# Two attention stages: gate tiles requested on ScalarE's DMA queue, five buffers in the local one, and all its low parts on GpSimd

## The reference

```
def _mixer_swa(h, positions, w_in, sinks):
    ...
    o = _banded_gqa(q, k, v, SWA_WINDOW, sinks).reshape(B, S, MIX_WIDTH)
    return o * jax.nn.silu(z)

def _mixer_mla(h, positions, w_in, q_norm, kv_norm, w_uq, w_ukv):
    ...
    o = _mla_attention(q_nope, q_rope, k_nope, k_rope, v).reshape(B, S, MIX_WIDTH)
    return o * jax.nn.silu(z)
```

## Time and profile before

| | us |
|---|---|
| median of 3 runs | 3240.16 (3235.90 to 3241.09) |
| profiled execution, its own time | 3234.05 |
| its span in the profile | 3232.2 |

### The profile page before, as it was taken

One profiled execution on the slowest core, in us unless ns is written; L12 is line 12 of the kernel. 1 busy time (PEld: TensorE's weight loads), 2 busy tenths in 40 slices (PEclk: granted clock), 3 DMA queues, 4 the chain that ended last, 5 costly groups with the idle time before them and its releaser, 6 DMA issues. The chain is left out here.

```text
span 3232.2 us, 40805 instructions
## 1 busy us (share of the span) xinstructions
PE 2960.0 (92%) x13514; PEld 2324.8 (72%) x13536; DVE 1913.8 (59%) x2771; ACT 1575.7 (49%) x2778; POOL 1244.5 (39%) x1044
## 2 busy tenths in 40 slices
PE   8999977778899999999677789999999999799998
PEld 6888875555688778888565467777777777578877
DVE  3544215444278774444555568778787787347875
ACT  3111114556444544444223167777777777544553
POOL 0022002223132541000210068888888888523353
PEclk9999988889899999999898789999999999899999
DMA  5255349664897665554567924252442522399764
GB/s 176 72 125 124 106 107 190 155 156 117 274 295 242 234 231 195 177 173 147 191 261 289 293 62 105 69 125 69 95 103 69 125 69 53 100 301 284 235 222 159
DMA packets 268849, 531.15 MB, mean 164 GB/s; under 512 B 46376, under 2 KB 94632, under 8 KB 260080
## 3 DMA queue, kind: packets, MB, share of 16 engines
q1 hardware_dynamic: 215696, 412.78, 44.5%
q10 hardware_dynamic: 52960, 116.02, 11.5%
HBM read 351.06 MB, written 177.37 MB: 163 GB/s over the span
## 5 line engine op out<-in xcount | busy, mean ns | idle before, releaser
L2161 POOL TENSOR_TENSOR mla_pl<-mla_p,mla_ph 128x512 fp32r<-128x512 f32 (+3 forms) x640 | 707.2, 1120 | 361.0 <-ACT mla_p L2023 352.5
L1324 PE MATMUL end_bank<-end_xh,end_whi 128*128 128x512 f32 x1600 | 633.1, 396 | 49.9 <-DVE end_xl L1510 28.7
L1325 PE MATMUL end_bank<-end_xl,end_whi 128*128 128x512 f32 x1600 | 625.0, 391 | 0.0
L1326 PE MATMUL end_bank<-end_xh,end_wlo 128*128 128x512 f32 x1600 | 625.0, 391 | 0.0
L1881 PE MATMUL mla_score<-mla_q,mla_k 96*128 96x512 f32 (+7 forms) x1920 | 555.7, 392 | 6.3 <-DMA mla_q<-mla_m_t 6.3
L1496 DVE TENSOR_TENSOR end_wlo<-end_wraw,end_whi 128x1024 fp32r<-128x1024 f32 x188 | 256.4, 1364 | 366.7 <-ACT end_whi L1379 366.2
L1379 ACT CAST end_whi<-end_wraw 128x1024 fp32r<-128x1024 f32 x188 | 197.2, 1049 | 552.8 <-PE end_bank L1326 516.2
L2022 ACT ACTIVATE mla_ph<-mla_score 128x512 fp32r<-128x512 f32 (+3 forms) x640 | 341.0, 533 | 225.8 <-PE mla_score L1881 222.8
L1881 PEld LDWEIGHTS mla_score<-mla_q,mla_k 96*128 96x128 f32 (+1 forms) x1920 | 362.8, 193 | 91.5 <-issue 36.8
L2053 DVE TENSOR_REDUCE mla_mx<-mla_mx 128x1 f32<-128x512 f32 (+3 forms) x640 | 371.9, 603 | 94.2 <-PE mla_mx L1881 93.6
L2099 DVE TENSOR_TENSOR mla_acc<-mla_acc,mla_p 128x512 f32<-128x512 f32 (+3 forms) x576 | 348.6, 605 | 118.6 <-ACT mla_p L2023 114.6
(11 more groups left out here) (233 smaller groups left out, 4695.7 us busy)
## 6 DMA issues: line engine op xcount, KB each, us to landing
end_wraw<-in_w_out ACTq DMA_DIRECT2D x64, 512.0 KB, 7.8
end_wraw<-in_pe_gate ACTq DMA_DIRECT2D x64, 512.0 KB, 4.8
end_wraw<-in_w_in ACTq DMA_DIRECT2D x56, 512.0 KB, 3.8
swa_q<-scratch_q_hi SPq DMA_DIRECT2D x32, 512.0 KB, 9.3
end_raw<-scratch_o SPq DMA_DIRECT2D x32, 512.0 KB, 11.7
end_factor<-scratch_inv SPq DMA_DIRECT2D x64, 256.0 KB, 10.0
scratch_proj<-end_out_f SPq DMA_DIRECT2D x64, 256.0 KB, 7.0
scratch_sum<-end_out_f SPq DMA_DIRECT2D x64, 256.0 KB, 6.5
```

Source lines behind the costliest of these rows:

```text
L1324: nc.tensor.matmul(bank, wh[:, at], xh[:, k0 + k, :], start=(k == 0), stop=False)
L1325: nc.tensor.matmul(bank, wh[:, at], xl[:, k0 + k, :], start=False, stop=False)
L1326: last = nc.tensor.matmul(bank, wl[:, at], xh[:, k0 + k, :], start=False, stop=(k == kc - 1))
L2161: pool.tensor_tensor(p_lo[b][:, off:TC], prob[b][:, off:TC], p_hi[b][:, off:TC].bitcast(F32), ALU.subtract).then_inc(p_lo_ok, 1)
```

## The change

1. The requests for gate tiles leave SP's program and go to ScalarE's. Before the first unit's work ScalarE requests the first `n_gate - 2` of them, and at the first step of a chunk c, ahead of its wait for the scores, that of chunk c + `n_gate - 3`.
2. `n_gate` is 5 in the local attention and 3 in the global one. The output tile and the denominator row keep three buffers.
3. `on_vector`, `low_part` and the second semaphore go: GpSimd makes the low part of every step in the local attention too.

```
-        small = 3
+        small, n_gate = 3, 3 if long else 5
...
-        def on_vector(g):
-            return not long and not flat[g][2]["last"]
...
-            def load_gate(c):
-                if c >= small:
-                    sp.wait_ge(gated, c - small + 1)
-                sp.dma_start(cfg["gate"](gate[c % small]), cfg["gate_src"](*chunks[c])).then_inc(gate_in[c % small], 16)
-
             load_high(0)
             load_low(0)
-            load_gate(0)
             load_high(1)
             for c in range(len(chunks)):
                 u = chunks[c][0]
-                if c + 1 < len(chunks):
-                    load_gate(c + 1)
                 if c == 0 or chunks[c - 1][0] != u:
...
-                if on_vector(g):
-                    pe.wait_ge(p_lo_v_ok, low_count[g])
-                else:
-                    pe.wait_ge(p_lo_ok, low_count[g])
+                pe.wait_ge(p_lo_ok, g + 1)
                 mm(out, v, low, False, st["last"]).then_inc(weighed, 1)
...
+            def load_gate(c):
+                if c >= n_gate:
+                    act.wait_ge(gated, c - n_gate + 1)
+                act.dma_start(cfg["gate"](gate[c % n_gate]), cfg["gate_src"](*chunks[c])
+                              ).then_inc(gate_in[c % n_gate], 16)
+
+            ahead = n_gate - 3
+            for c in range(ahead + 1):
+                load_gate(c)
             max_row(0)
             for g in range(total + tail):
                 if g < total:
...
+                    if st["first"] and c and c + ahead < len(chunks):
+                        load_gate(c + ahead)
                     act.wait_ge(scores, g + 1)
...
             for g in range(total + tail):
-                if g < total and not on_vector(g):
+                if g < total:
```

More of the change, by code:

```diff
@@ L1735, in attention_phase @@
         den_row = [s.sb(f"den_row{b}", [1, TC]) for b in range(small)]
-        gate = [s.sb(f"gate{b}", [HEAD_DIM, TC]) for b in range(small)]
+        gate = [s.sb(f"gate{b}", [HEAD_DIM, TC]) for b in range(n_gate)]
         o_out = [s.sb(f"o_out{b}", [HEAD_DIM, TC]) for b in range(small)]
@@ L1752, in attention_phase @@
         mrow = [s.sem(f"max_row{b}") for b in range(2)]
-        gate_in, stored, den_stored = ([s.sem(f"{n}{b}") for b in range(small)]
-                                       for n in ("gate_in", "stored", "den_stored"))
-        (const_ok, scores, probs, p_lo_ok, p_lo_v_ok, acc_init, summed, weighed, mx_prod, mx_done, m_done, m_turned,
+        gate_in = [s.sem(f"gate_in{b}") for b in range(n_gate)]
+        stored, den_stored = ([s.sem(f"{n}{b}") for b in range(small)] for n in ("stored", "den_stored"))
+        (const_ok, scores, probs, p_lo_ok, acc_init, summed, weighed, mx_prod, mx_done, m_done, m_turned,
          m_t_ok, low_ok, sum_ok, den_ok, row_ok, gated) = (s.sem(n) for n in (
-             "const_ok", "scores", "probs", "p_lo_ok", "p_lo_v_ok", "acc_init", "summed", "weighed", "mx_prod", "mx_done",
+             "const_ok", "scores", "probs", "p_lo_ok", "acc_init", "summed", "weighed", "mx_prod", "mx_done",
              "m_done", "m_turned", "m_t_ok", "low_ok", "sum_ok", "den_ok", "row_ok", "gated"))
@@ L2099, in add @@
                 vec.tensor_tensor(into[:, both], acc_ps[:, both], now[:, both], ALU.add).then_inc(summed, 1)
[L2101 to L2106, removed]
             def finish(c):
@@ L2116, in out_gate @@
                 dve.wait_ge(weighed, last_of[c] + 1)
-                dve.wait_ge(gate_in[c % small], 16 * (c // small + 1))
+                dve.wait_ge(gate_in[c % n_gate], 16 * (c // n_gate + 1))
                 if c >= small:
                     dve.wait_ge(stored[c % small], 16 * (c // small))
-                vec.tensor_tensor(o_out[c % small][:], o_ps[c % 2][0:HEAD_DIM, :], gate[c % small][:], ALU.mult
+                vec.tensor_tensor(o_out[c % small][:], o_ps[c % 2][0:HEAD_DIM, :], gate[c % n_gate][:], ALU.mult
                                   ).then_inc(gated, 1)
@@ L2129, in _ @@
                     u, k, st = flat[g]
-                    if on_vector(g):
-                        low_part(g)
                     for n in at_slot(u, k):
@@ L2148, in out_gate @@
                 pool.wait_ge(sum_ok, c + 1)
-                pool.wait_ge(gate_in[c % small], 16 * (c // small + 1))
+                pool.wait_ge(gate_in[c % n_gate], 16 * (c // n_gate + 1))
                 if c >= small:
                     pool.wait_ge(stored[c % small], 16 * (c // small))
-                pool.tensor_tensor(o_out[c % small][:], o_sum[c % 2][:], gate[c % small][:], ALU.mult
+                pool.tensor_tensor(o_out[c % small][:], o_sum[c % 2][:], gate[c % n_gate][:], ALU.mult
                                    ).then_inc(gated, 1)
             for g in range(total + tail):
-                if g < total and not on_vector(g):
+                if g < total:
                     off, b = flat[g][2]["off"], g % nbuf
```

## The result

The changed kernel takes 3204.06 us in the median of four runs (3195.64 to 3213.30) against 3239.58 for the kernel before: ratio 0.9893, 95% interval 0.9869 to 0.9917, so 35.5 us less, between 27 and 42. On another chip, beside the experiments, the ratio was 0.9904 (0.9887 to 0.9920). Forecast were 3211 us and a gain of 28.4. The experiments ran on three chips, each beside the kernel before (3237.9 to 3239.4 us in the median), and their ratios are to that; between chips it is the ratios that compare.

A forecast was written before the change was run, and what follows sets the result against it. Local attention was taken to be bound by late gate loads behind SP's burst, global attention by TensorE. Terms -28.5 (stall), -2.3 and +2.4 (ends), others 0, sum to -28.4: from 3240.2 to 3211.8, say 3211 us; range 3184 to 3234.

The forecast's parts named there:

- what the stall is worth: Local attention, five units of chunks 6 to 46: 212.2 us against 157.2 without stalls, so 55.0 us to win.
- The backlog moves to the stores: ScalarE's queue during SP's burst: gates and stores share it, so chunks wait for the output tile's store instead of gates.
- Its place: Late stores would hold chunks 9 and 10, or chunks 17 and 18 in a unit starting with a one-block chunk.
- Its size: Slips of 4.5 us in three units and 6.5 in two: 26.5 us of stall stay, 28.5 won.
- About 55 packets per us: Assumed rate of ScalarE's queue in the burst's long-piece part: one store or gate per 4.7 us or more.
- The low parts at nothing: Local attention's 60 subtractions moved from VectorE to GpSimd: price 0, or +13 us if short steps lack slack.
- The ends of the stages: First late gate gone, -2.3 us; gates beside the first loads +1.8 at most, global attention's start +0.6.
- The issues on ScalarE and its new wait at nothing: 64 gate requests per attention on ScalarE, about 0.6 us each, hidden: 0, otherwise up to +19 us; new wait 0.
- A (the stall goes): Rival: queue shares fairly, slips of 1 us a unit, gain 49.9 us, 3190 us; chance 0.20.
- B (the stall keeps its size): Rival: gate wait becomes a store wait of 10.5 us a unit; 3238 us, no change; chance 0.12.
- ends -2.4: Term for the stage ends in the rival where the stall keeps its size, added to -2.5 to give 3238 us.
- C (the queue fills and holds ScalarE): Rival: ScalarE's queue fills and stops its exponentials, 8 us a unit on top; +11.5, 3252 us; chance 0.07.

The follow-up runs named there:

- after_out5: The changed kernel with five instead of three buffers for the output tile and denominator row in local attention; 3177.7 us, ratio 0.9806 to the kernel before.
- after_again: The changed kernel itself, unaltered, measured once more beside the experiments; 3207.0 us, ratio 0.9904 to the kernel before.
- global_gates_only: The kernel before with only the global attention's gate requests moved to ScalarE's queue; 3237.3 us, ratio 0.9994.
- after_gate6: The changed kernel with a sixth gate buffer in local attention, requests at the same places; 3206.8 us, ratio 0.9909 to the kernel before.
- after_gate3: The changed kernel with three gate buffers instead of five in local attention; 3203.9 us, ratio 0.9896 to the kernel before.

## Why the prediction was right, and where not

**What bounds the kernel, and what the stall is worth.** Right. A unit without stalls was put at 30.6 and 32.0 us, and after_out5 shows 29.8 to 30.5 and 32.5 at a clock of 1.00. The 55.0 us that were to be won are 54.4 there (212.2 - 157.8).

**The backlog moves to the stores.** The mechanism was right: no gate waits, stores behind gates in one queue (landing 10.0, 14.5 and 14.6 us after their issue at 534.85, 537.18 and 542.11), the output tile as the new limit. That it was the store was tested both ways: two more buffers give 29 us after the change and nothing before.

**Its place was wrong.** I had chunks 9 and 10; it is 7, 8 and 9. I let SP start the burst 2 us earlier against the chunks. It was 1.3 us behind the gating of chunk 6 (541.93 against 540.61) and is 3.7 us ahead (533.82 against 537.56), 5 us. The exponential at 539.78, which I took for the last step of the unit, belongs to the second of the next; the unit's last score was done at 535.8. In the unit that starts with a one-block chunk I had chunks 17 and 18; it is 17, with 7.4 us in place of 3.6.

**Its size.** 26.5 us were to stay in the five units; 180.4 - 157.2 = 23.2 stayed, and 27.2 in after_again. That this agrees is luck in good part, for the working under it was off twice, in opposite directions. I had four transfers on ScalarE's queue land between 541 and 562.5. Nine land between 536.9 and 560.2, because the burst starts earlier against the chunks; but they take 2.6 us each, where I had 4.7 for the long pieces. VectorE's waits for stores in a unit were to be 3 to 5 us and are 7.4 to 11.1; TensorE's waits behind them are 17.3 us in all, and what a unit lost is 3.7 to 5.7 us.

About 55 packets per us was not a rate that the queue has. The 272 packets in 547 to 552 are one store (256 packets) and little more, and nearly nothing moved from 550 on. SP's queue and ScalarE's in 550 to 553, kernel before:

```profile
q1 hardware_dynamic: 181, 0.66, 104.0%
q10 hardware_dynamic: 8, 0.00, 0.4%
```

Nor was it merely what the stores asked for: a store was outstanding all the time from 542.81 to 564.9, and they landed 8.4, 10.7, 12.2 and 8.9 us after issue. What the rows show is standstills beside a waiting store, as here, and between them turns of equal count with SP's queue: 225 packets against 246 in 558 to 562 in the kernel before, 237 against 235 and 201 against 204 after. After the change, in this burst, the queue stood still from 537 to 540 and then no more. Why the standstills come, and why there are fewer with more waiting, is open.

**The low parts at nothing: wrong.** I asked whether GpSimd could keep up, and it does (3.5 us of waits). I did not ask what stands behind VectorE's low part in its program. It was the gating, and in the short steps taking the subtraction out made it 2.5 us earlier. The move is worth 6 us alone and 11 beside the gates, and a gain was in none of the prices that I gave it. The sum came out near because of this: the gates alone bring 20 us (3237.9 - 3217.9), not 28.4. So the forecast of the time was nearer than its terms, by luck.

The prediction looked for a standstill of one engine beside the other in GpSimd's times only. VectorE's show something like it. In the kernel before:

```profile
538.25 1.29 POOL L2161 TENSOR_TENSOR swa_pl<-swa_p,swa_ph 128x512 fp32r<-128x512 f32 x1 [2.64 <-ACT swa_p L2023]
539.19 0.90 DVE L2106 TENSOR_TENSOR swa_pl<-swa_p,swa_ph 128x512 fp32r<-128x512 f32 x1 [1.41 <-ACT swa_p L2023]
```

Of VectorE's 60 subtractions at least 15 start while one of GpSimd's runs. With 0.35 us of overlap they take 0.90 us, with 0.23 to 0.26 us 0.78 to 0.81, with 0.16 and less 0.69 to 0.70, as alone. In sum that is about 2 us of VectorE's time, too little to be the gain.

**The ends of the stages.** The first late gate went: chunk 0 to 6 takes 21.9 us where it took 23.9 (forecast 2.3). The start, from SP's first load to the first gating, is 0.9 us longer (forecast 1.8 at most). Global attention is 2.1 us shorter in the one pair of traces, where nothing was forecast; global_gates_only shows no gain there.

**The issues on ScalarE and its new wait at nothing.** Right, by global_gates_only and after_gate6, though the trace of the changed kernel alone, with its 36.4 us, would have said otherwise.

**The rivals.** A (the stall goes) came true only with the output buffers. B (the stall keeps its size) did not. Its "ends -2.4" is a slip: -2.3 and +2.4 make +0.1, which is what gives 3238. C (the queue fills and holds ScalarE) shows nowhere: no issue of a gate took over 0.9 us in the local attention (1.6 in the global one), while SP was held 7.1 to 9.7 us in issuing a burst's last load in four of the units from 570 us on.

The Trainium skill (DMA: Bandwidth & Descriptors, Queues, rings and completion order) has each engine drain whole packets, of up to 64 descriptors, from one queue before it switches to the next. The equal counts of the two queues (235 and 237, 204 and 201) agree with turns. How large a turn is they don't show, and turns don't account for 8 packets beside 181. So where the prediction says that the trace agrees, with no bytes for 4 us and then one transfer per 4.7 us, it claims more than its rows show.

## What to carry to other kernels

A mean number of packets per us is not yet a queue's rate: look at when something was waiting in it, cut the stretch finer, and hold it against the other queue on the same engines. When an instruction leaves an engine that is not the bound, look at what stood behind it in program order, not at the busy time it frees. And when late loads are moved into the queue of the stores, give the stores' tiles more buffers in the same step: here that was worth nearly as much again as the change, 3178 us in place of 3207. Without them, earlier requests in the old queue did better than the new queue.

## What the runs showed of the hardware

Beside a burst on SP's queue, ScalarE's queue moved packets one for one with it (237 and 235, 201 and 204, 244 and 246), whether SP's were of 3.8 KB or of 0.7 KB; and for some 3 us at a time it moved next to nothing with a store waiting (8 against 181 in 550 to 553 us of the kernel before). A subtraction of VectorE's that started beside one of GpSimd's took up to 0.90 us in place of 0.69, and GpSimd's took 1.26 to 1.30 throughout. The granted clock was 0.91 to 1.00 in units with TensorE waits of 5 us and less, 0.84 to 0.88 in those with 9.2 to 9.5, and 1.00 in units without. The changed kernel's runs spread more (3195.6 to 3213.3) than those of after_gate3 (3202.5 to 3205.6); why is open.
